# Expert rows gathered in 1 KB pieces and turned on VectorE instead of TensorE, in a routed encoder layer on one Trainium2 core

## What is computed

```python
# 4 groups of 4 experts; each token goes to 2 experts of its best group
hid = silu(t @ w_gate[e]) * (t @ w_up[e])      # 1024 -> 512
out = out + combine[:, e] * (hid @ w_down[e])  # 512 -> 1024
# then: x = x + sigmoid(norm(x) @ w_ple_gate) * (p @ w_ple_proj); norm(x)
```

## Time and profile before

| | |
|---|---|
| median of 3 runs | 639.49 us (637.5 to 639.87) |
| the profiled execution, its own time | 636.99 us |
| its span (first to last instruction) | 635.1 us |
| PE busy | 589.0 us, 93% |
| DVE, ACT, POOL busy | 209.7, 199.0, 51.1 us |
| traffic | 151.52 MB, mean 239 GB/s |
| PE's mean granted clock | 0.967 of full |

### The profile page before, as it was taken

The page is one execution under the profiler, slowest core; times in us unless marked ns, Lnnn a source line. Parts: engine busy times, 40 slices in busy tenths (PEclk is TensorE's granted clock), DMA queues, the critical chain, the costliest instruction groups (busy, mean ns, idle before and its releaser), DMA issues.

```text
span 635.1 us, 9546 instructions
## 1 busy us (share of the span) xinstructions
PE 589.0 (93%) x3496; PEld 386.2 (61%) x3497; DVE 209.7 (33%) x460; ACT 199.0 (31%) x435; POOL 51.1 (8%) x89
## 2 busy tenths in 40 slices
PE   9999999999999999975769999999999987998994
PEld 9988777878988999974223333333333332335883
DVE  4521365456344342265101111011011010164753
ACT  5622254545443543240100010010010010073774
POOL 0000000000000000001101211211212211110000
PEclk9999999999999999995789999999999999998998
DMA  9852214213220249737994799999999999934001
GB/s 310 221 203 99 71 63 133 67 32 101 68 67 1 67 160 419 316 136 296 362 418 183 296 418 425 422 418 422 419 422 422 420 421 421 393 120 179 34 33 66
DMA packets 47232, 151.52 MB, mean 239 GB/s; under 512 B 7896, under 2 KB 27232, under 8 KB 34656
## 3 DMA queue, kind: packets, MB, share of 16 engines
q1 hardware_dynamic: 43520, 139.77, 56.3%
q0 software_dynamic: 3392, 11.02, 4.4%
q10 hardware_dynamic: 288, 0.29, 0.2%
HBM read 141.62 MB, written 9.45 MB: 238 GB/s over the span
## 4 chain that ended last, share of the span: by engine, by line
PE 83%; DMA 5%; DVE 4%; issue 3%; SPq 2%; ACT 2%; DVEq 0%; POOL 0%; ACTq 0%; POOLq 0%
PE bank L1622 19%; PE bank L1348 13%; PE bank L1349 12%; PE bank L1350 12%; PE bank L1648 10%; DMA ring_dn<-in_w_down 5%; PE bank L1430 2%; PE bank L1681 2%; SPq L586 2%; PE bank L1608 2%; PE bank L1403 2%; PE bank L1356 1%; PE bank L1634 1%; PE bank L1567 1%; PE bank L1444 1%
## 5 line engine op out<-in xcount | busy, mean ns | idle before, releaser
L1622 PE MATMUL bank<-ring_gu,rowsT 128*64 128x512 f32 (+1 forms) x800 | 144.7, 602 | 6.4 <-DMA ring_gu<-in_w_up 2.8
L1622 PEld LDWEIGHTS bank<-ring_gu,rowsT 128*64 128x64 f32 (+1 forms) x800 | 43.9, 128 | 92.4 <-issue 88.1
L1648 PE MATMUL bank<-ring_dn,hidT 128*64 128x512 f32 (+1 forms) x400 | 74.7, 607 | 9.8 <-issue 5.2
L891 ACT ACTIVATE silu_g<-bank 128x256 f32<-128x256 f32 x20 | 7.7, 384 | 221.8 <-PE bank L1622 221.8
L1087 DVE TENSOR_TENSOR w_lo<-w_raw,w_hi 128x2048 fp32r<-128x2048 f32 x17 | 39.0, 2293 | 76.7 <-ACT w_hi L752 64.9
L1246 DVE TENSOR_TENSOR hid<-silu_g,bank 128x256 f32<-128x256 f32 x20 | 8.4, 421 | 147.9 <-ACT silu_g L891 147.9
L1348 PE MATMUL bank<-w_hi,hT_hi 128*128 128x256 f32 x192 | 55.5, 289 | 0.8 <-issue 0.6
L1349 PE MATMUL bank<-w_lo,hT_hi 128*128 128x256 f32 x192 | 54.3, 283 | 0.0
L1350 PE MATMUL bank<-w_hi,hT_lo 128*128 128x256 f32 x192 | 54.3, 283 | 0.0
L1348 PE MATMUL bank<-hT_hi,w_hi 128*128 128x512 f32 x128 | 50.9, 397 | 0.1
L1648 PEld LDWEIGHTS bank<-ring_dn,hidT 128*64 128x64 f32 (+1 forms) x400 | 21.0, 128 | 48.4 <-issue 42.3
(11 more groups left out here) (217 smaller groups left out, 892.7 us busy)
## 6 DMA issues: line engine op xcount, KB each, us to landing
ring_gu<-in_w_gate SPq DMA_DIRECT2D x32, 1024.0 KB, 12.3
ring_gu<-in_w_up SPq DMA_DIRECT2D x32, 1024.0 KB, 15.3
ring_dn<-in_w_down SPq DMA_DIRECT2D x16, 2048.0 KB, 21.5
w_raw<-in_w_in SPq DMA_DIRECT2D x13, 1024.0 KB, 5.0
w_raw<-in_w_out SPq DMA_DIRECT2D x4, 1024.0 KB, 4.9
ple_gate_raw<-in_w_ple_gate SPq DMA_DIRECT2D x1, 4096.0 KB, 28.9
yg<-y_rows SPq DMA_DIRECT2D x8, 512.0 KB, 7.2
xr<-in_x SPq DMA_DIRECT2D x4, 512.0 KB, 8.8
```

Of the source, the lines that this page charges most:

```text
L1622: last = T.matmul(b_gu[q * BLK + t:q * BLK + t + n, :], rowsT[:, k % 4, k // 4, t:t + n], ring_gu[s][:, :, k, q * UC:(q + 1) * UC], start= ...
L1648: last = T.matmul(b_dn[q * BLK + t:q * BLK + t + n, :], hidT[:, kf % 2, kf // 2, t:t + n], ring_dn[s][:, kf, q * (D // 2):(q + 1) * (D // 2)],
```

## The change

1. `h2_rows` becomes rows of 256 values (1 KB), four to a token (QUADS). A gather brings in one group of 32 slots: partition 32c+s holds quarter c of slot s. A block takes two gathers, so `src_row` has a column per group (56 in place of 28), and the offset and one-hot arithmetic in the routing follows (32-slot marks; `dst_row` is made in four instructions of 32 partitions).
2. DVE turns the rows: one `transpose` instruction of 128x512 elements, which turns each 32x32 square by itself, writes `rowsT`. The four PE transposes and ACT's copy go. It waits until gate_up of the block before is done, since there is one `rowsT`.
3. DVE turns `hid` with eight transposes of 32 partitions x 128 elements, after it has copied the y of the block before. The two PE transposes and DVE's copy go.
4. Because squares are turned and not the whole tile, a partition of `rowsT` holds 8 neighbouring values of the contracted index (8p to 8p+7), and one of `hidT` 4. The weights are loaded to match: partition p holds rows 8p to 8p+7 of gate and up (a half load is still 8 KB per partition, now with a pitch of 16 KB), and rows 4p to 4p+3 of down (16 KB in one run, before two runs of 8 KB).

```diff
-                    src = w[bass.ds(e, 1)].rearrange("o (q p j) f -> p (o q) j f", p=P, q=2)
+                    src = w[bass.ds(e, 1)].rearrange("o (p h j) f -> p (o h) j f", p=P, h=2)
...
-                sp.dma_start(ring_dn[slot][:].rearrange("p (q j) n -> p q j n", q=2),
-                             w_down[bass.ds(e, 1)].rearrange("o (q p j) n -> p (o q) j n", p=P, q=2)).then_inc(s_dn[slot], 16)
+                sp.dma_start(ring_dn[slot][:],
+                             w_down[bass.ds(e, 1)].rearrange("o (p j) n -> p (o j) n", p=P)).then_inc(s_dn[slot], 16)
...
             for buf in range(ROW_BUFS):
-                sp.wait_ge(s_rows[buf], 16)
+                sp.wait_ge(s_rows[buf], 32)
             load_dn(2, 2)
...
+            def gather(buf, table, first):
                 pool.sem_inc(gathers_begun, 1)
-                pool.indirect_dma_start(out=rows[buf][:], out_offset=None, in_=h2_rows,
-                                        in_offset=rows_of).then_inc(s_rows[buf], 16)
+                for g in range(2):
+                    rows_of = bass.IndirectOffsetOnAxis(ap=table[:, first + g:first + g + 1].bitcast(U32), axis=0)
+                    pool.indirect_dma_start(out=rows[buf][:, g, :], out_offset=None, in_=h2_rows,
+                                            in_offset=rows_of).then_inc(s_rows[buf], 16)
...
             def step(b, k, turn):
-                pool.wait_ge(xT_done, b + 1)
+                pool.wait_ge(xT_ready, b + 1)
...
-            def rowsT_evac(b):
-                act.wait_ge(xT_done, b + 1)
-                nc.scalar.activation(rowsT[:], b_xT[:]...
...
+                of_group = b_rows[1].rearrange("p (b g) -> p b g", g=2)
+                for c in range(QUADS):
+                    quad = slice(c * GRP, (c + 1) * GRP)
+                    last = V.tensor_scalar(dst_row[quad], of_group[quad, :, c % 2], row_offset[quad, 1:2], None, ALU.add)
+                last.then_inc(rows_ready, 1)
...
+            def hidden_turned(b):
+                dve.wait_ge(hid_ready, b + 1)
+                for c in range(QUADS):
+                    q, g = divmod(c, 2)
+                    for h in range(2):
+                        last = V.transpose(hidT[(2 * q + h) * GRP:(2 * q + h + 1) * GRP, :, g * GRP:(g + 1) * GRP],
+                                           hid[c * GRP:(c + 1) * GRP, h * P:(h + 1) * P].rearrange("p (d m) -> p m d", m=4))
+                last.then_inc(hidT_ready, 1)
+
+            def rows_turned(b, buf, loads):
+                dve.wait_ge(s_rows[buf], 32 * loads)
+                if not isinstance(b, int) or b:
+                    dve.wait_ge(gu_done, b)
+                V.transpose(rowsT[:].rearrange("p k (g s) -> p g k s", g=2),
+                            rows[buf][:].rearrange("p g (d k) -> p g k d", k=KD)).then_inc(xT_ready, 1)
+
+            rows_turned(0, 0, 1)
+            rows_turned(1, 1, 1)
             hidden(0)
+            hidden_turned(0)
             for b in range(2):
-                hiddenT(b)
+                rows_turned(b + 2, b, 2)
                 hidden(b + 1)
                 evacuate_y(b, b, fresh=True)
+                hidden_turned(b + 1)
             def step(b, k, turn):
-                hiddenT(b + 1)
+                rows_turned(b + 3, k % 2, (GROUP // 2) * turn + (k + 4) // 2 + 1)
                 hidden(b + 2)
                 evacuate_y(b + 1, k % 2)
+                hidden_turned(b + 2)
...
             def step(b, k, turn):
-                hidden_transpose(b - 1)
+                pe.wait_ge(hid_ready, b)
                 gate_up(b)
-                with pe.If(turn % ROW_BUFS < 1):
-                    rows_transpose(0, turn // ROW_BUFS + 2)
-                with pe.Else():
-                    rows_transpose(1, turn // ROW_BUFS + 2)
                 down(b - 1)
```

More of the change, by code:

```diff
@@ L236, in trunk @@
         p_sb = at("p_sb", 16, [P, NT, D_PLE])
-        rows = [at(f"rows{i}", 64 + 2 * i, [P, D // 2]) for i in range(ROW_BUFS)]
-        rowsT = at("rowsT", 68, [P, 4, 2, BLK])
+        rows = [at(f"rows{i}", 64 + 2 * i, [P, 2, D // QUADS]) for i in range(ROW_BUFS)]
+        rowsT = at("rowsT", 68, [P, KD, BLK])
         silu_g = at("silu_g", 70, [P, UC])
         hid = at("hid", 71, [P, UC])
-        hidT = at("hidT", 72, [P, 2, 2, BLK])
+        hidT = at("hidT", 72, [P, D_EXPERT // P, BLK])
         y_blk = [at(f"y_blk{i}", kb, [P, D // 2]) for i, kb in enumerate((73, 76, 101.25))]
@@ L299, in trunk @@
         w_top = [tiny(f"w_top{k}", [P, NT]) for k in range(2)]
-        src_row = tiny("src_row", [P, TABLE], I32)
+        src_row = tiny("src_row", [P, GROUPS], I32)
         dst_row = tiny("dst_row", [P, TABLE], I32)
-        src_now = [tiny(f"src_now{i}", [P, 1], I32) for i in range(3)]
+        src_now = [tiny(f"src_now{i}", [P, 2], I32) for i in range(3)]
         dst_now = [tiny(f"dst_now{i}", [P, 1], I32) for i in range(3)]
@@ L381, in trunk @@
         in_blk = at("in_blk", 45.25, [P, 2 * NT])
-        blk_oh = at("blk_oh", 100.5, [P, 2 * NT, TABLE])
-        blk_rows = at("blk_rows", 68, [P, 2, 2 * NT, TABLE])
+        blk_oh = at("blk_oh", 100.5, [P, 2 * NT, GROUPS])
+        blk_rows = at("blk_rows", 68, [P, 2, 2 * NT, GROUPS])
         slot_oh = at("slot_oh", 203.75, [P, 2 * NT, P])
@@ L693, in scatter @@
                 pool.wait_ge(s_ystored, 16 * (b + 1))
[L694 removed]
+                columns(dst_now[buf], dst_row, b, 1)
                 pool.wait_ge(column_ready, n_columns)
                 pool.sem_inc(scatters_begun, 1)
+                rows_of = bass.IndirectOffsetOnAxis(ap=dst_now[buf][:].bitcast(U32), axis=0)
                 pool.indirect_dma_start(out=y_rows, out_offset=rows_of, in_=y_blk[buf][:],
@@ L1038, in rows_in_blocks @@
                 def rows_in_blocks(w):
[L1039 to L1043, removed]
+                    return V.tensor_tensor(blk_rows[:, w], blk_oh[:], wide(rows_of_pair[:, w], GROUPS), ALU.mult)
+                link(V.tensor_scalar(blk_r[:], pairs, 0.5 - GRP / 2, ROUND_GRP, ALU.add, ALU.add))
+                V.scalar_tensor_tensor(in_blk[:], blk_r[:], -ROUND_GRP, pairs, ALU.add, ALU.subtract)
+                link(V.tensor_tensor(blk_oh[:], wide(blk_r[:], GROUPS), all_pairs(grp_marks), ALU.is_equal))
                 rows_in_blocks(0)
@@ L1602, in column_tiles @@
                 return [(q, g * GRP, GRP, slots[g]) for g in range(2) for q in range(2)]
-            def rows_transpose(buf, loads):
-                pe.wait_ge(s_rows[buf], 16 * loads)
-                for j in range(4):
-                    last = T.transpose(b_xT[:, j * P:(j + 1) * P], rows[buf][:, j::4], ident)
-                last.then_inc(xT_done, 1)
             def gate_up(b, pairs=ANY):
@@ L1621, in products @@
                         for q, t, n, s in column_tiles(slots):
-                            last = T.matmul(b_gu[q * BLK + t:q * BLK + t + n, :], rowsT[:, k % 4, k // 4, t:t + n],
+                            last = T.matmul(b_gu[q * BLK + t:q * BLK + t + n, :], rowsT[:, k, t:t + n],
                                             ring_gu[s][:, :, k, q * UC:(q + 1) * UC],
@@ L1629, in gate_up @@
                 in_slots(b, products, pairs)
-            def hidden_transpose(b):
-                pe.wait_ge(hid_ready, b + 1)
-                for j in range(2):
-                    last = T.transpose(b_hT[:, j * P:(j + 1) * P], hid[:, j::2], ident)
-                last.then_inc(hT_done, 1)
             def down(b, pairs=ANY):
```

67 lines of the change are left out of this document (26 added, 41 removed).

## The result

| | before | after |
|---|---|---|
| median, same chip, 20 runs each | 638.94 us (636.9 to 640.72) | 641.05 us (637.93 to 645.35) |
| ratio after / before | | 1.0039, 95% interval 1.002 to 1.0057 |
| profiled execution, its own time | 636.99 us | 645.35 us |
| its span | 635.1 us | 643.5 us |

The change makes the kernel 0.4% slower (0.2% to 0.6%): no difference by the bound of 0.5%, as forecast, though the interval reaches just past that bound. The two traces stand 8.4 us apart where the medians stand 2.1 apart: the one of before is 2 us quicker than its median, the one of after 4.3 us slower. Where it matters a second trace of the changed kernel stands beside it (a1_again, an execution of 642.72 us).

The account below looks back on a forecast made before the run. The prediction took the full DMA weight stream to bound the blocks; start -1.6, pieces +2.3, layout -0.3 and tail -0.4 summed to 0.0, put on the median: 639.5 us, own range 636.5 to 642.5, wider range 632.0 to 646.0.

Parts of the forecast that it names:

- What bounds: Blocks: the full DMA weight stream sets their end; PE merely keeps pace, so most removed transpose time becomes waiting for weights.
- PE was the bound after all: Rival, blocks: PE bounds and the 22 us of removed transposes come through, about 618 us; chance 0.04.
- The start: From the routing tables to SP's issue at 353.02 us: the full weight stream starts 1.6 us earlier, bounds -6 and +2.
- I leave them as they are: First pass through PE's loop: the issue stalls of 1.58, 5.16 and 1.16 us were taken as unchanged.
- -2.2 us: Ahead of 353 us: rows transposes of blocks 2 and 3 and hidden transposes of blocks 1 and 2 removed from PE.
- The 1 KB pieces: Gathers in the full stream: smaller pieces cost +0.146 us each over 16 blocks, +2.3 us, between 0 and +10.4.
- Pieces are dear: Rival, gathers: the price goes by piece count, +10.4 us in place of 2.3, about 646 us; chance 0.18.
- The layout: Down weight loads in the stream: 16 KB runs save at most 0.6 us, taken as -0.3.
- After the last load: From the last down weights to the last down: 17.6 us against 18.0, -0.4 us (-1.4 to +2.1).
- PE falls to the lower clock: Rival, PE after waits: a slow down behind the last load costs 1.8 us, two 3.6; about 643 us; chance 0.06.
- Cover in mid-loop: Steady loop: DVE's turns fit under PE's down and gate_up at no cost; the next gather has over 4 us to spare.
- Faster at the start: Rival, first pass: the 5.16 us stall falls to 1.2 and pieces are free, about 633 us; chance 0.24.

Follow-up runs that it names:

- b3: Changed kernel, loading only 256 bytes per partition of down weights from expert 3 on: 616.88 us, ratio 0.9645 to the kernel before.
- b4: Kernel before, loading only 256 bytes per partition of down weights from expert 3 on: 630.25 us, ratio 0.9866 to the kernel before.
- a4_hold: Changed kernel, SP holding back expert 3's down weights (2 MB) until half of the third gate_up is done: 642.48 us, ratio 1.0052 to before.
- b1_hold_both: Changed kernel, SP holding back 4 MB of gate and up and 2 MB of down until half of the third gate_up: 643.3 us, ratio 1.0076 to before.
- a3_tail: Changed kernel, last block's hid turned before y is copied, into its own buffer: 638.49 us, ratio 1.0007 to before.
- c3_old_layout: Changed kernel with weights laid out as in the kernel before, so products mix wrong rows and weights: 644.38 us, one execution.
- c1_start_tail: Changed kernel, block 0's rows turned before the small routing work, and last block's hid before copying y: 637.66 us, ratio 1.0006 to before.
- c4_plain_turn: Changed kernel with DVE's turns reading neighbouring values instead of every eighth or fourth, so values land wrongly: 638.54 us, one execution.
- c2_start_tail_warm: c1_start_tail plus 16 unused products on TensorE behind the table products: 633.05 us, ratio 0.9915 to before.

## Why the prediction was right, and where not

As a whole it was right: 641.05 us against 639.5, in the own range of 636.5 to 642.5, and in the class "within 0.5%". The stream hides PE's saving, as said, and b3 and b4 show it. That the sum came within 1.6 us is in part luck, for its terms were not right one by one:

- **What bounds.** Right. PE's block is 10.6 us, the DMA share 1.0 from 375 us on, and the page puts 13.5 us of waiting of `down` on its weights; from 375 to 540 us PE waits 18.3 us for weights in all, where about 15 were forecast. *PE was the bound after all* falls.
- **The start, "-1.6 us".** Its first step, +1.3 us to the first gate_up, was too small: +3.0 and +2.5 in the two traces. The tables are ready 1.9 us later in place of 1.1 (`dst_row` at 243 ns an instruction, 1.02 for the four; some 0.4 stood already at the start of the routing; 1.4 later in a1_again), small instructions and register loads together took 2.75 in place of 2.3, the turn 1.11 in place of 0.7. The step that failed is "I leave them as they are", of the first-pass stalls, together with the -2.2 us of removed transposes: PE's stall there ends near the last code packet, whatever PE had to do before (a4_hold, b1_hold_both), so what is taken out of PE's work ahead of it turns into stall. 5.16 became 8.27, and the upper bound of +2 us left too little room for that. From the end of the second gate_up to the start of the third it is 14.2 us (327.86 to 342.01) and 12.8 in a1_again, against 12.8 before, though two transposes are gone and `down` ran at 4.2 us in place of 5.38. The -0.7 between the first and the second gate_up did not come either: the gap is 3.8 us against 3.1. And the third gate_up ran at the lower clock, 2.1 us longer (2.8 in a1_again), all of it ahead of expert 5's issue. Only the last 1.1 of the 2.2 us came through. In sum the issue is 5.6 us later (4.5 in a1_again) for the forecast -1.6.
- **What a late issue is worth.** I measured the stream from one issue of SP. b1_hold_both shows that this holds only while nothing else is shifted: the sum of idle DMA time ahead of it is the quantity.
- **How large the start is in the median** stays open. The traces say +4.5 to +5.6 us for the issue of expert 5. But they compare an execution of before that is 2 us below its median with two of after that lie 1.7 and 4.3 above theirs. From the medians, +2.1 less 2.5 for the tail (a3_tail) less about 1 for the stream leaves about -1.4, with at least 2 us of uncertainty. The other traces with the same start speak for a loss: expert 5 is issued at 355.06 (a3_tail), 355.72 (a4_hold), 356.61 (c3_old_layout) and 358.35 us (b3_after_light), against 352.60 in b4_before_light, whose start is that of before. So the start is 2 to 6 us later in every pair, and how that goes with the medians is not known.
- **The 1 KB pieces, "+2.3 us".** Too dear. The term that was mis-sized is the price of 48.6 engine-us per MB, taken from 1 KB runs of another queue. q0's went from 39.7 to 40.4 for gathers and scatters together; if scatters kept theirs, gathers pay about 41, +0.02 us a block, 0.4 us in all. By the Trainium skill, "DMA: Bandwidth & Descriptors", "Specifications" (512 B is enough for line rate), it would be nothing; on this queue the trace agrees with the page, and the row that I weighed against it does not carry over. *Pieces are dear* falls. From expert 5's issue to the end of the stream it is 203.0 us before and 203.5 to 204.8 with the change; the 0.1 to 1.4 us beyond the pieces are not explained.
- **The layout, "-0.3".** Not told apart from nothing (c3_old_layout).
- **After the last load, "-0.4 us".** It was +2.1, the upper bound. The eight turns took 3.24 us in place of 2.3, mostly for the stride, and the last `down` took 5.35 for 3.65, at a lower granted clock behind a wait of 4.22. That was the content of the rival *PE falls to the lower clock*, at its place and price of 1.8 us for one `down`; it did not come in the place of the forecast but on top. a3_tail takes the slow clock away and a part of the wait.
- **Cover in mid-loop.** Right: the turns, the second gather and the copies lie beside PE's work; PE waits there for weights, not for `rowsT` or rows.
- **Faster at the start.** Its lever exists (b1: the stall at 2.79 us), but what it gives back in PE is not given back by the stream.

The sum of the terms was right by errors that offset each other, which is luck: pieces 1 to 2 us too dear, the tail 2.5 us too cheap, the start by the two traces 6 to 7 us too early, by the medians uncertain.

## What to carry to other kernels

Where a stream of weights sets the end, add up the idle time of the DMA engines ahead of it rather than following one issue: work taken off PE, or a load held back, pays only if it lowers that sum. What lies behind the last load is paid in full, so there look at the order of every step, engine by engine; here the order of two steps was worth 2.5 us, about as much as the whole change cost. And it is worth trying to keep TensorE from standing idle just before a stage that others wait for: here 6 us of products with no use bought 4.6 us, of which the first stage behind them accounts for 1.1.

## What the runs showed of the hardware that was not expected

- DVE's transpose of 32x32 squares of 4-byte values takes 1.11 us for 128x512 read at every eighth value and 0.71 read in a row; 0.40 and 0.30 for 32x128 at every fourth.
- Instruction code moves as 16 KB packets through the same 16 DMA engines. While these were full of weights, five packets came mostly 6 us apart, once they were empty 3 to 4 us; PE's stall ahead of the third gate_up was 8.27 and 7.99 us with the engines full (after, a1_again) and 2.79 with them empty (b1_hold_both).
- A PE that was kept busy until 0.17 us ahead of a product ran it in 7.09 us; behind 5.99 us of idle time (c1_start_tail) the same product took 8.87. At the tail, `down` took 5.35 us behind a wait of 4.22 or 3.49 us (after, c4_plain_turn) and 3.65 behind one of 2.55 (a3_tail). The length of the last wait alone does not decide it: the `down` behind the last down weights took 5.35 us behind 1.96 us of waiting in a4_hold and 3.65 behind 1.95 in a3_tail.
- The last stage, which no kernel here touches, took 58.4 or 60.0 us from the first x transpose to the end (a1_again and c2_start_tail_warm: 58.4; before and after: 59.9 and 60.0). That is about 1.5 us of the spread between single executions.
